# Attention and the output mix written as one program, with the output weights prepared during the last head

## The reference, cut to what matters

```python
q, k, v, logf, gate_b, cu = project(rms(x) , w_in, b_f)
o_attn = softmax(q.k/8 + decay, causal) @ v            # 512 columns
o_conv = gate_b * causal_conv3(cu)                     # 512 columns
merged = concat(rms(o_attn, g_attn_out), rms(o_conv, g_conv_out))
x  = x + rms(merged @ w_o, g_post_mix)
m  = square(relu(rms(x, g_pre_mlp) @ w_up)) @ w_down
x  = x + rms(m, g_post_mlp)
```

## Time and profile before

| | us |
|---|---|
| median of 3 runs | 2872.6 |
| runs | 2870.83, 2872.60, 2876.43 |
| the profiled execution | 2872.0 |
| its span in the trace | 2870.3 |
| last product with values of the attention | 1110.4 |
| first product of the mix | 1134.0 |
| first product of the mix's tile 1 | 1154.4 |
| last product of the mix | about 1356.8 |

### The profile page before, as it was taken

The page is one execution under the profiler, slowest core; times in us unless marked ns, Lnnn a source line. Parts: engine busy times, 40 slices in busy tenths (PEclk is TensorE's granted clock), DMA queues, the critical chain, the costliest instruction groups (busy, mean ns, idle before and its releaser), DMA issues.

```text
span 2870.3 us, 40267 instructions
## 1 busy us (share of the span) xinstructions
PE 2736.9 (95%) x14550; PEld 2408.4 (84%) x14550; DVE 1264.7 (44%) x2362; ACT 894.8 (31%) x1621; POOL 896.9 (31%) x573
## 2 busy tenths in 40 slices
PE   7999999999999996999799999999999999999997
PEld 6899899898787785887699999999987888888886
DVE  4333444238887886676232323232244322222235
ACT  3201301117787775454211111111122211211212
POOL 3233334311001111443333333333345333333343
PEclk9999999999999998999899999999999999999999
DMA  5543544665543464468601010111164111111113
GB/s 176 192 129 107 159 109 136 209 179 120 135 106 96 111 151 135 148 199 237 190 30 59 29 58 29 58 33 55 40 182 156 45 58 45 44 45 58 44 44 117
DMA packets 277187, 305.24 MB, mean 106 GB/s; under 512 B 36220, under 2 KB 238472, under 8 KB 272456
## 3 DMA queue, kind: packets, MB, share of 16 engines
q1 hardware_dynamic: 226808, 260.47, 31.3%
q10 hardware_dynamic: 37744, 25.96, 2.8%
q0 software_dynamic: 12512, 17.30, 2.3%
HBM read 221.21 MB, written 82.21 MB: 106 GB/s over the span
## 4 chain that ended last, share of the span: by engine, by line
PE 47%; DMA 2%; POOL 2%; DVE 1%; ACT 0%; issue 0%; SPq 0%; POOLq 0%; DVEq 0%
PE up_bank L2351 24%; PE dn_bank L2374 23%; DMA m_x_in<-scratch_x 1%; POOL y L2169 1%; DMA m_h_lo<-scratch_h_lo 0%; DVE y L2305 0%; POOL dn_lo L2149 0%; POOL up_lo L2149 0%; DMA m_raw<-in_w_down 0%; DMA m_x_in<-y 0%; POOL u_hl L2161 0%; DVE y L2292 0%; POOL m_h_hi L2141 0%; DVE up_lo L2308 0%; ACT dn_hi L2220 0%
## 5 line engine op out<-in xcount | busy, mean ns | idle before, releaser
L2374 PE MATMUL dn_bank<-dn_hi,u_hl 128*128 128x512 f32 x2112 | 671.8, 390 | 6.6 <-DVE y L2290 4.4
L2161 POOL TENSOR_TENSOR u_hl<-u,u_hl 128x64 fp32r<-128x64 f32 (+2 forms) x192 | 200.0, 1064 | 901.3 <-DVE u L2277 901.3
L2374 PEld LDWEIGHTS dn_bank<-dn_hi,u_hl 128*128 128x128 f32 x2112 | 397.3, 188 | 90.4 <-DVE y L2290 4.8
L2351 PE MATMUL up_bank<-m_h_hi,up_hi 128*128 128x512 f32 (+2 forms) x1280 | 451.6, 353 | 18.3 <-DVE up_lo L2308 11.3
L2351 PE MATMUL up_bank<-m_h_hi,up_lo 128*128 128x512 f32 (+2 forms) x1280 | 451.2, 352 | 0.0
L2351 PE MATMUL up_bank<-m_h_lo,up_hi 128*128 128x512 f32 (+2 forms) x1280 | 451.1, 352 | 0.0
L2230 ACT ACTIVATE u<-up_bank 128x512 f32<-128x512 f32 (+2 forms) x160 | 83.7, 524 | 1158.4 <-PE up_bank L2351 1152.3
L2292 DVE TENSOR_TENSOR y<-dn_bank,y 128x1024 f32<-128x1024 f32 x255 | 312.1, 1224 | 289.1 <-PE dn_bank L2374 289.0
L2374 PE MATMUL dn_bank<-dn_lo,u_hl 128*128 128x512 f32 x1088 | 425.0, 391 | 0.0
L2277 DVE TENSOR_TENSOR u<-u 128x512 f32<-128x512 f32 (+2 forms) x160 | 94.0, 629 | 696.5 <-ACT u_hl L2233 696.5
L504 POOL TENSOR_TENSOR w_lo<-w_raw,w_hi 128x1024 fp32r<-128x1024 f32 x72 | 181.2, 2521 | 336.2 <-DVE w_hi L722 336.2
(11 more groups left out here) (255 smaller groups left out, 4760.0 us busy)
## 6 DMA issues: line engine op xcount, KB each, us to landing
w_raw<-in_w_in SPq DMA_DIRECT2D x72, 512.0 KB, 4.2
m_raw<-in_w_up SPq DMA_DIRECT2D x32, 1024.0 KB, 5.5
m_raw<-in_w_down SPq DMA_DIRECT2D x32, 1024.0 KB, 4.9
nck<-scratch_ncum SPq DMA_DIRECT2D x9, 1312.0 KB, 18.4
scratch_v_hl<-vhl SPq DMA_DIRECT2D x20, 512.0 KB, 2.7
q_hi<-scratch_q_hi SPq DMA_DIRECT2D x18, 528.0 KB, 7.6
q_lo<-scratch_q_lo SPq DMA_DIRECT2D x18, 528.0 KB, 9.4
v_hl<-scratch_v_hl SPq DMA_DIRECT2D x9, 1024.0 KB, 20.9
```

The source lines that it names most:

```text
L2161: rest = pool.tensor_tensor(u_hl[:, o % 2, b, to], u[:, b, at], u_hl[:, o % 2, b, at].bitcast(F32), ALU.subtract)
L2351: mm = pe.matmul(up_bank[2 * (o % 2) + b][:, 0:w], wp[:, c, k, b * P:(b + 1) * P], hp[g][s][:, k, :], start=(k == 0 and p == 0), stop=(k = ...
L2374: mm = pe.matmul(bank[:, cols], u_hl[:, o % 2, b, part], wp[:, c, b, cols], start=(b == 0 and p == 0), stop=(b == 1 and p == len(passes) - 1))
```

## The change

**One block.** `attend` no longer makes its own block: it writes its queues into a block that `mix_rows` goes on with, so the barrier and the fresh start of every engine between them are gone. Each engine passes from its attention code to its mix code by an unconditional branch.

**The last iteration written out.** The loop runs three times, and heads 6 and 7 follow as straight code (`final`). It leaves out the scores, exponentials and loads of the head that does not exist.

**Weights.** A new class `MixFront` places the mix's tiles over memory that the attention has finished with. In the place of the loads of that unused head, SP loads all eight blocks of `w_o` into the buffers of head 6. POOL, not ACT and DVE, splits them: a rounded copy (`tensor_copy`) and a subtraction in place for each, two behind group 0 of head 7, one behind the sample rows, three behind group 1 and two behind group 2.

**First rows.** `load_first` (the first tiles' rows, `g_conv`, `g_attn`) waits until all scores are taken. `g_conv` is now loaded directly as 128x4 with single elements of 4 bytes, and not loaded as rows and turned on PE. POOL forms `cg` and the sum of squares of tile 0 before it closes group 2, `c_lo` after the last two splits. DVE blanks rows and forms `ag` between the `p_lo` of group 3, ACT forms `c_hi` there.

**TensorE.** Behind the last product with values: the transposes of `ag`, half of the products of `c_bank`, the four transposes of the last N, the sum of squares, the other half of `c_bank`, all of `a_bank`, and the transposes of tile 1. The rest of the mix and the MLP stay as they were, apart from where their tiles lie.

The core of the diff:

```diff
+SPLITS = {(1, QT // 4): (4,), (1, 0): (5, 6), (1, 1): (7, 0, 1), (1, 2): (2, 3)}
@@ attend: loop
-            with eng.Fori(0, HEADS // 2) as it:
+            with eng.Fori(0, AGAIN) as it:
                 for x in queue_of(body, name):
                     step(it, x)
+            for x in queue_of(final, name):
+                step(AGAIN, x)
+        AGAIN = HEADS // 2 - 1
+        final = [x for x in body if x.off < 2 or x.kind == "L"]
@@ attend: sync
+                if x is wide_o and isinstance(it, int):
+                    sp.wait_ge(used, P_BUFS + upto("V", it, x.v.at) + 1)
+                    front.load_rows(sp)
+                if x is last_max and isinstance(it, int):
+                    sp.wait_ge(taken, ALL_TAKEN)
...
+                    front.load_first(sp)
...
+                if isinstance(it, int) and x.off == 2:
+                    front.load_weights(sp)
+                    return
@@ attend: gpsimd
+                if x.kind == "N" and not (last and x is last_n):
+                    close(it, x)
+                    if last and (x.off, x.g) in SPLITS:
+                        for k in SPLITS[x.off, x.g]:
+                            front.split_weights(pool, k)
+                if last and x is last_turns[0]:
+                    pool.wait_ge(taken, ALL_TAKEN)
+                    front.set_ones(pool)
+                    front.conv_first(pool)
+                if last and x is last_turns[8]:
+                    front.conv_first_rest(pool)
@@ attend: scalar and vector
+                if isinstance(it, int) and x is last_turns[6]:
+                    front.conv_first_hi(act)
+                if isinstance(it, int) and x is last_o:
+                    front.squares_first(act)
...
+                    if isinstance(it, int) and x is last_turns[1]:
+                        dve.wait_ge(turned, 1 + upto("T", it, last_turns[0].at))
+                        front.blank_rows(dve)
+                    if isinstance(it, int) and x is last_turns[8]:
+                        front.scale_first(dve)
@@ class MixFront
+    def split_weights(self, pool, k):
+        pool.wait_ge(self.w_loaded[k], 16)
+        pool.tensor_copy(self.w_hi[:, k, :], self.w_raw[:, k, :]).then_inc(self.S["w_hi_done"], 1)
+        self.n_split += 1
+        pool.wait_ge(self.S["w_hi_done"], self.n_split)
+        pool.tensor_tensor(self.w_lo[:, k, :], self.w_raw[:, k, :], self.w_hi[:, k, :].bitcast(F32), ALU.subtract).then_inc(self.S["w_lo_done"], 1)
+    def load_first(self, sp):
+        conv = self.dr["conv_t"].rearrange("(j p) r -> p j r", p=P)
+        sp.dma_start(self.c_in[:, 0, :, 0:DEC], conv[:, :, SEQ:ROWS]).then_inc(self.c_loaded[0], 16)
+        sp.dma_start(self.g_conv[:, :], self.io["g_conv_out"].rearrange("o (j p) -> (o p) j", p=P),
+                     allow_slow_non_contiguous=True).then_inc(self.S["g_loaded"], 16)
...
@@ mix_rows: tensor
+            last_rows["scores_free"]()
             turn(0, 0)
+            pe.wait_ge(S["w_lo_done"], CJ)
+            pe.wait_ge(S["c_lo_done"], 1)
+            multiply(c_bank, c_hi, c_lo, 0, CJ, S["c_mult"], (0,))
+            last_rows["pe"]()
+            last_rows["turns_free"]()
+            pe.wait_ge(S["ones_done"], 1)
+            sum_squares(0)
+            multiply(c_bank, c_hi, c_lo, 0, CJ, S["c_mult"], (1,))
+            pe.wait_ge(S["w_lo_done"], KB)
+            pe.wait_ge(S["a_lo_done"], 1)
+            multiply(a_bank, a_hi, a_lo, 0, 0, S["a_mult"])
+            turn(1, 1)
+            sum_squares(1)
```

375 lines of the change are left out of this document (213 added, 162 removed).

## The result

| | before | after |
|---|---|---|
| median | 2873.5 (4 runs, 2870.8 to 2876.4) | 2851.0 (4 runs, 2850.4 to 2852.4) |
| span of the profiled execution | 2870.3 | 2848.7 |
| first product with values of the attention | 649.4 | 646.0 |
| start of the last scores that are used | 1091.5 | 1094.1 |
| last product with values | 1110.4 | 1114.5 |

The time is 0.9925 of the time before, with a 95% interval of 0.9913 to 0.9936: 22.5 us less, where 28.0 were forecast. The time lies 6.4 us above the forecast and at the upper end of the range.

What follows compares the result with a forecast made beforehand. TensorE's products through the MLP bound the kernel; starting tile 1's `a_bank` products at 1126.4, not 1154.4, gains 28.0 us: 2872.0 to 2844.0, plus 0.6 for the median, 2844.6 us. Range 2840.5 to 2851.

Steps and rivals of the forecast that it cites:

- the mark: Start of the first `a_bank` product of tile 1 in the mix, at 1154.42 before; forecast at 1126.4.
- One end of a loop iteration goes away too: Attention's loop: one jump back fewer, worth 0.8 us, bounds 0 to 1.7.
- the memsets and `ag`: Last group of the attention: this DVE work ahead of a `p_lo` costs PE 0.8 us, bounds 0 and 2.0.
- the scores taken out: Last group on PE: five score pieces of a nonexistent head go, saving 2.2 us, bounds 1.5 and 2.5.
- it may wait out one POOL operation: From the slower rival, chance 0.02: `ag` on DVE may wait 2.5 us, while PE waits for `c_lo` anyway.
- POOL was to be the bound: Start of the mix: PE's first product waits for POOL's `c_lo` and may start at 1112.0.
- the gains landed as forecast: Loads behind the last scores: gains there at 1097.8, so POOL can begin; bounds 1096.5 to 1100.
- the rival's, PE bound through DVE: Start of the mix: rival with `c_lo` at 1109.7, PE barely pausing, time 2841.4; chance 0.10.
- `g_conv` in single elements: Late-gains rival: this load lands 1.2 us later, `c_lo` comes at 1115.2, time 2850 to 2852; chance 0.12.
- The wait for `part`: Before tile 1's `a_bank` products: transposes, then ACT's copy, root and `part` with nothing over them, 3.4 us.
- The clock: a rival: PE's pauses before `c_lo` and before tile 1's `a_bank`: clock falls, 2 us each, 2846.6 or 2848.6; chance 0.30.
- 12.7 us per tile: The mix's later tiles: each keeps this length, since nothing there is queued otherwise than before.

Runs made afterwards that it cites:

- e1_counter: Changed kernel with DVE's waits ahead of the loop counted in a register again, six instructions put back; 2843.4 us, ratio 0.9894.
- e4_ag_early: Changed kernel with the three blank-row memsets on POOL and DVE forming `ag` three `p_lo` earlier; 2850.2 us, ratio 0.9925.
- e7_unrolled: Changed kernel with the attention's loop of three written out, so no engine jumps back in it; 2837.1 us, ratio 0.9874.
- e3_order: Changed kernel with the second half of tile 0's `c_bank` products behind `a_bank` and tile 1's transposes on PE; 2849.4 us, ratio 0.9919.
- r1_after: The changed kernel as it is, profiled a second time; attention 447.2 us, where the first profile had 448.1.
- e12_unrolled_best: Changed kernel with the loop written out, `c_bank` split around `a_bank`, blank rows on POOL, `ag` and `c_lo` early; 2832.3 us, ratio 0.9861.
- e10_pad248: Changed kernel with 248 single-column memsets of an unused tile ahead of the loop on DVE; no median given, stall of 1.33 us at the second jump.

## Why the prediction was wrong, and where it was right

The forecast span was 2842.3, the measured one 2848.7. The difference of 6.4 us by the steps of the prediction, from the first pair of profiles:

| step | forecast | measured | off by |
|---|---|---|---|
| first product with values | 649.4 | 646.0 | -3.4 |
| attention | 441.3 | 448.1 | +6.8 |
| last scores to the mix's first product | 20.5 | 20.9 | +0.4 |
| from there to the mark | 15.2 | 15.1 | -0.1 |
| behind the mark | 1715.9 | 1718.6 | +2.7 |

**The attention: the step that failed.** "One end of a loop iteration goes away too" was costed, with 0.8 us and bounds of 0 to 1.7, and that was about right, if low: against the kernel before, e1_counter gains 1.8 us, with two cheap jumps and one fall through. What the sum took for granted is that the two jumps that stay cost what they had cost. They cost 7.9 us more together (448.1 against 440.3), since the diff also replaces six register instructions on DVE, ahead of the loop, by constants. I had read that as an edit without a price. No row of the trace before shows it, but the order of the instructions does show that the loop's head moves by six places, and with a jump on the path that is a reason for a bound of its own: it would have put the range's upper end near 2859 (2851 and the 7.9 measured since).

**DVE in the last group: a term too small.** For the memsets and `ag` I put 0.8 us on PE (bounds 0 and 2.0), and for the scores taken out 2.2 (bound 1.5). e4_ag_early measures both: without memsets and with a short `ag` on DVE the last product with values is 17.5 us behind the scores, so the scores are worth about 1.4 (18.9 before), and the memsets and the blocked `ag` cost 2.9. About half of that is the block: in e7_unrolled, with the memsets on DVE and `ag` free by luck of the moment, it is 18.9, although the clock fell there. The sentence "it may wait out one POOL operation, 2.5 us, while PE has `c_lo` to wait for anyway" was right in its first half (2.61) and wrong in the second, because of the next point.

**What bounds PE there: the wrong one of two.** POOL was to be the bound, with `c_lo` ending 20.4 us behind the last scores. It ended 19.8 behind them: the gains landed as forecast, and of the two rounded copies one took 1.04 us, not 1.5, and the other 1.49 only because `ag` held it. PE came 3 us later than forecast. So the two errors nearly cancel (0.4 us), but the mechanism is the rival's, PE bound through DVE, at a time that the rival did not have. e4_ag_early brings POOL's bound back at once. The estimate of 0.9 us from the Trainium skill's GPSIMD Engine Reference (section 3.1, "Elementwise") was nearer than the value that I took; the trace's 1.04 is 0.1 above it. Loads, splits and closings in head 7 stayed hidden, as said; `g_conv` in single elements was not late.

**The wait for `part`: right.** 3.4 us from tile 1's transposes to its first product, forecast and measured (1126.76 to 1130.13). e3_order shows that it can be covered whole. The products ahead of it were to take 11.8 us and took 11.7 (1115.02 to 1126.76).

**The clock: a rival that comes by chance.** In the changed kernel's first profile only the second of the two pauses came, and the clock stayed up. It fell in that pause in r1_after, e1_counter, e4_ag_early and e7_unrolled, where tile 1's products take 6.9 to 7.2 us in place of 5.6. Its price of 1.3 to 1.6 us was a little under the 2 I gave. What I had not seen is that it falls behind the gaps of the two jumps.

**Behind the mark: not unchanged.** "12.7 us per tile" was wrong in the kernel's favour: 12.53, 3.3 us in all. Against it stand 2.0 us on the way to the MLP, where ACT is held longer by the issue of its store of `h_lo` (5.13 us against 4.17; over the merged profiles but e12's the way takes 23.5 to 24.2 us where that issue takes up to 4.3, and 25.2 to 26.1 where it takes 4.7 to 5.4), and 3.9 us in the MLP, above all at the start of its second group of rows. ACT's line near the end of the mix, after and before, and PE's at the start of that group, after and before:

```profile
1333.16 1.09 ACT L1806 ACTIVATE h_hi<-h_bank 128x512 fp32r<-128x512 f32 x2 [7.17 <-DMA scratch_h_lo<-h_lo]
```

```profile
1358.69 1.08 ACT L1667 ACTIVATE h_hi<-h_bank 128x512 fp32r<-128x512 f32 x2 [5.51 <-DMA scratch_h_lo<-h_lo]
```

```profile
2167.00 0.80 PE L2480 MATMUL up_bank<-m_h_hi,up_hi 128*128 128x512 f32 x1 [3.08 <-POOL up_lo L2278]
```

```profile
2190.74 0.49 PE L2351 MATMUL up_bank<-m_h_hi,up_hi 128*128 128x512 f32 x1 [1.52 <-POOL up_lo L2149]
```

POOL is late behind loads that land later (23.2 us for five in its chain, 22.3 before). e12_unrolled_best has hardly any of both losses (24.5 us on the way, 1.75 at this place, 1440.3 for the MLP), with the same tiles in the same places; so it is not the tiles' place alone. Why the issue and the loads take longer is open.

**The start.** The first product with values came 3.4 us sooner than before, in the second pair of profiles 3.8. But the merged kernels lie between 645.2 and 648.8 (655.2 with its 248 memsets) and the kernel before and its variants between 646.5 and 649.9, so part of it at least is chance: in both profiles of the kernel before the clock had fallen in a stretch near 45 us, in those of the changed one not. That is luck in the forecast's favour: with the start at 649.4 the time would have been 3.4 us further above it.

## What to carry to other kernels

In these runs the price of a loop's jump back depended on where the head lies: when a diff adds or drops even a few instructions ahead of a loop, compare the idle time of each engine at the jump, and look for one that is put down to issue. The same `ag` took from 0.68 to 2.75 us, by what ran on POOL beside it, so give a product of two SBUF tiles on DVE a place beside POOL's waits and not beside its work. When two chains end within a microsecond or two of each other, cost the second as carefully as the first, for it decides what a fix of the first is worth.

## What the runs showed of the hardware

- A jump to a loop's head on DVE: at most 2.8 to 3.1 us of idle time at one place of the head (2.45 without any jump), 5.1 to 5.6 at another up to three instructions earlier. At the second kind of place one more packet of 8192 bytes starts on an instruction queue before the first operation, about 2 us behind the one before it; with 248 instructions put in ahead of the loop (e10_pad248) the first score comes in time and a stall of 1.3 to 1.4 us follows, eight or nine instructions into the body. Six instructions fewer made the kernel before 0.36% slower.
- An operation of DVE with two SBUF inputs is stopped by a two-input operation of POOL that has started (0.69 becomes 2.61 us beside one of 2.38, and 1.80 beside one of 1.29), and POOL by one of DVE: its copy took 1.49 in place of 1.04, and a subtraction 2.75 in place of 2.4 when `ag` had started 0.2 us ahead of it. The Trainium skill's SBUF — State Buffer ("SBUF: two separate sides") says that whichever of the two starts first holds the shared ports for its whole length and the other waits; it sets no number of inputs for POOL's side, so the copy, which I had not expected to wait, falls under it too. The traces agree.
- In the pause of 2.66 us before tile 1's `a_bank` products the granted clock stayed at 1.00 in four profiles and fell to 0.50 in four; of two executions of the same program it fell in one.
- In the mix, products of 128x512 stand 0.233 us apart in one program and down to 0.227 in another with the same instructions; neither the order of the PSUM banks nor that of the weights in SBUF explains it.
